# Twenty of the later modulation units moved from TensorE's stream to VectorE, in X's space

## The reference, cut to what matters

```
def adaln(cond, w, b):
    m = jax.nn.silu(cond) @ w + b            # w: (2048, 6 * 2048) per layer
    return six vectors of 2048: shift, scale, gate for the mixer and for the MLP
h  = modulate(x, g, shift, scale)            # rmsnorm(x, g) * (1 + scale) + shift
x  = x + gate * rmsnorm(mixer(h), g1)
m  = square(relu(modulate(x, ...) @ w1)) @ w2    # w1: 2048 x 8192, w2: 8192 x 2048
x  = x + gate * rmsnorm(m, g3)
```

## Time and profile before

| | |
|---|---|
| median of 3 runs | 2559.13 us (2557.03 to 2560.53) |
| profiled execution | 2560.89 us; its span 2559.1 us |
| TensorE busy (matmul) | 2497.7 us, 98% of the span |
| VectorE, ScalarE, GpSimd busy | 1364.3, 1050.2, 114.5 us |
| DMA moved | 634.51 MB, mean 248 GB/s |
| MLP0, MLP1 (first to last up-projection start and on) | about 560 to 1340 us, 1830 to 2559 us |

### The profile page before, as it was taken

The page is one execution under the profiler, slowest core; times in us unless marked ns, Lnnn a source line. Parts: engine busy times, 40 slices in busy tenths (PEclk is TensorE's granted clock), DMA queues, the critical chain, the costliest instruction groups (busy, mean ns, idle before and its releaser), DMA issues.

```text
span 2559.1 us, 37169 instructions
## 1 busy us (share of the span) xinstructions
PE 2497.7 (98%) x14658; PEld 2023.2 (79%) x14658; DVE 1364.3 (53%) x1492; ACT 1050.2 (41%) x1148; POOL 114.5 (4%) x164
## 2 busy tenths in 40 slices
PE   6899999989999999999999999999999999999998
PEld 3578888778778778778887777797787888888887
DVE  2244544475446545545565455565765465565565
ACT  3223334363333333333453365584633333343343
POOL 0020000000000000000000023200000000000000
PEclk8999999999999999999999999999999999999999
DMA  9989888958888887887867954457588555555554
GB/s 361 361 265 297 281 290 281 350 182 277 304 267 270 285 299 247 280 303 244 277 239 256 315 171 165 157 196 273 184 258 282 190 189 205 167 194 197 187 196 175
DMA packets 493365, 634.51 MB, mean 248 GB/s; under 512 B 12128, under 2 KB 370320, under 8 KB 491984
## 3 DMA queue, kind: packets, MB, share of 16 engines
q1 hardware_dynamic: 484576, 608.46, 71.3%
q0 software_dynamic: 6352, 23.31, 2.7%
q10 hardware_dynamic: 2336, 1.31, 0.2%
HBM read 623.90 MB, written 9.13 MB: 247 GB/s over the span
## 4 chain that ended last, share of the span: by engine, by line
PE 79%; DMA 10%; DVE 5%; ACT 4%; issue 2%; SPq 0%; ACTq 0%; DVEq 0%
PE PS L1301 23%; PE PS L1304 12%; PE PS L1371 11%; PE PS L1372 10%; PE PS L1373 10%; PE PS L1330 5%; DVE WLO L1864 3%; DMA RAW<-in_w_qkvg_gla 3%; ACT WHI L1608 2%; DMA RAW<-in_w_o_na 2%; DMA RAW<-in_w_o_gla 2%; DMA SCR<-in_w_ada 1%; DMA RAW<-in_w_qkv_na 1%; DMA RAW<-in_w_mlp 1%; PE PS L1484 1%
## 5 line engine op out<-in xcount | busy, mean ns | idle before, releaser
L1864 DVE TENSOR_TENSOR WLO<-RAW,WHI 128x2048 fp32r<-128x2048 f32 x384 | 879.1, 2300 | 776.1 <-ACT WHI L1608 767.4
L1608 ACT ACTIVATE WHI<-RAW 128x2048 fp32r<-128x2048 f32 x384 | 731.2, 1913 | 746.4 <-DMA RAW<-in_w_mlp 503.6
L1301 PE MATMUL PS<-HM,WHI 128*128 128x512 f32 x2560 | 650.8, 396 | 6.9 <-DVE SCR L2102 4.4
L1301 PEld LDWEIGHTS PS<-HM,WHI 128*128 128x128 f32 x2560 | 461.7, 189 | 105.8 <-issue 22.0
L1371 PE MATMUL PS<-WHI,HID 128*128 128x512 f32 x1152 | 454.0, 394 | 5.4 <-DVE WLO L1864 5.4
L1372 PE MATMUL PS<-WLO,HID 128*128 128x512 f32 x1152 | 449.7, 390 | 0.0
L1373 PE MATMUL PS<-WHI,HID 128*128 128x512 f32 x1152 | 449.1, 390 | 0.0
L1304 PEld LDWEIGHTS PS<-HM,WLO 128*128 128x128 f32 x2560 | 349.8, 191 | 25.8
L1304 PE MATMUL PS<-HM,WLO 128*128 128x256 f32 x2560 | 357.2, 283 | 0.0
L1371 PEld LDWEIGHTS PS<-WHI,HID 128*128 128x128 f32 x1152 | 216.6, 188 | 62.5 <-issue 17.9
L1373 PEld LDWEIGHTS PS<-WHI,HID 128*128 128x128 f32 x1152 | 216.8, 188 | 45.6
(11 more groups left out here) (239 smaller groups left out, 1691.5 us busy)
## 6 DMA issues: line engine op xcount, KB each, us to landing
RAW<-in_w_mlp SPq DMA_DIRECT2D x256, 1024.0 KB, 6.2
ADW<-in_w_ada SPq DMA_DIRECT2D x176, 1024.0 KB, 8.2
RAW<-in_w_qkv_na SPq DMA_DIRECT2D x48, 1024.0 KB, 7.1
RAW<-in_w_qkvg_gla SPq DMA_DIRECT2D x32, 1024.0 KB, 7.1
SCR<-in_w_ada SPq DMA_DIRECT2D x16, 1024.0 KB, 11.2
RAW<-in_w_o_na SPq DMA_DIRECT2D x16, 1024.0 KB, 7.2
RAW<-in_w_qkvg_gla SPq DMA_DIRECT2D x32, 512.0 KB, 4.7
RAW<-in_w_o_gla SPq DMA_DIRECT2D x16, 1024.0 KB, 6.5
```

What stands on the lines that cost most here:

```text
L1301: return mm(bank[:, 0:2 * T2], hi[:, k, P * b:P * b + P], act[:, kc, 0:2 * T2], start=first, stop=False)
L1608: actv(WHI[:, 2 * s + u, 0:n], RAW[:, u, 0:n], ACT.Copy).then_inc(hi_done, 1)
L1864: tt(WLO[:, 2 * s + u, 0:n], RAW[:, u, 0:n], WHI[:, 2 * s + u, 0:n].bitcast(f32), ALU.subtract).then_inc(lo_done, 1)
```

## The change

Units are still numbered 0 to 95, but 20 places among them are done in five "quads" of 4 units (1024 columns): after the out half's own units in groups 0, 1 and 2 of MLP0 and in groups 0 and 1 of MLP1. The last two quads overlap by one unit, so 19 different units leave TensorE's stream: 4 in the out half of each of groups 0 to 2 of MLP0, which keeps one unit in each of blocks 0 and 1, and all 7 of group 0 of MLP1. `ada` arguments become pairs (number in the stream, number of the unit), SKIP = 12 apart later on.

A quad q has 16 tiles of 128 rows by 1024 columns (512 KB). POOL loads each in two transfers of 256 KB into one of two slots, and VectorE multiplies it with the conditioning of its 128 rows, once for each vector, and adds it to two accumulators QACC (128 x 1024). Both the slots and the accumulators lie in X, which POOL parks in DRAM before and brings back after. TensorE sums QACC over the partitions with 8 matmuls, ACT copies and stores the rows.

```diff
+        PU = NB + 2
+        QU = 4
+        GU = PU + QU
+        QUADS0, QUADS1 = HID_GROUPS - 1, 2
-        PLAN_MLP = {GU: ((0, 1), (2, 3), (4,), (5,)), LU: ((0,), (1,), (2,), ())}
+        PLAN_MLP = ((0,), (1,), (), ())
+        QACC = [XF[:, QN * b:QN * b + QN] for b in range(2)]
+        QTILE = [XF[:, 2 * QN + QH * q:2 * QN + QH * q + QH] for q in range(2 * QN // QH)]
+        UP_TILES, OUT_TILES = 2 * NB, 2
+        QUAD_SLOT = [k % 2 for k in range(KC)]
...
         @block.tensor
...
+            def quad_rows(q):
+                pe.wait_ge(quad_step, q * KC + (KC + 1))
+                pe.wait_ge(quad_row, q + 1)
+                for b in range(2):
+                    for j in range(QU):
+                        end = mm(ROWS_TB[32 * j:32 * j + 32, 0:UC], PICK[b], QACC[b][:, UC * j:UC * j + UC],
+                                 start=(b == 0), stop=(b == 1))
+                end.then_inc(quad_summed, 1)
+                def between(n, x):
+                    planned_ada(None if a is None else g * PU + (a + NB), PLAN_MLP)(n, x)
+                    if quads is not None and n == YN - 1 and x == 2:
+                        quad_rows(g + quads)
...
         @block.scalar
...
+            def quad_store(q, unit):
+                act.wait_ge(quad_summed, q + 1)
+                act.wait_ge(quad_out, q * (16 * QU) + 16)
+                actv(QROW, ROWS_TB[:, 0:UC], ACT.Copy).then_inc(quad_row, 1)
+                act.wait_ge(quad_row, q + 2)
+                for j in range(QU):
+                    act.dma_start(mod_rows[ds(unit + j, 1)].rearrange("o h b j n -> (o b j) h n"),
+                                  QROW[32 * j:32 * j + 8, :].rearrange("p (h n) -> p h n", h=2)).then_inc(quad_out, 16)
...
         @block.vector
...
+            def quad_tile(q, k, slot, at):
+                dve.wait_ge(quad_zero, q * 2 + 2)
+                dve.wait_ge(quad_in[slot], q * (32 * PER_SLOT[slot]) + (at * 32 + 32))
+                dve.wait_ge(quad_step, q * KC + (k + 1))
+                for b in range(2):
+                    scale = CS[:, ds(k, 1), b:b + 1].rearrange("p o n -> p (o n)")
+                    end = nc.vector.scalar_tensor_tensor(QACC[b], QTILE[slot], scale, QACC[b], ALU.mult, ALU.add)
+                end.then_inc(quad_step, 1)
...
                 split_lo(m + 1, 1)
+                quad_out_tile(quad, n, 0)
...
                 split_lo(m + 2, 0)
+                for x in range(1, OUT_TILES):
+                    quad_out_tile(quad, n, x)
...
                     split_lo(slab + 1, 1 - s)
+                    if quad is not None:
+                        quad_tile(quad, i * 2 + s, s, i)
                     for b in range(2):
                         dve.wait_ge(hid_done, k + b + 1)
...
         @block.gpsimd
...
+            def quad(q):
+                if q:
+                    pool.wait_ge(quad_summed, q)
+                for b in range(2):
+                    nc.gpsimd.memset(QACC[b], 0.0).then_inc(quad_zero, 1)
+                for k in range(KC):
+                    slot, before = QUAD_SLOT[k], QUAD_BEFORE[k]
+                    if before is not None:
+                        pool.wait_ge(quad_step, KC * q + before + 2)
...
+                    for first, last in ((unit, middle), (middle, end)):
+                        at, col = (first - unit) * UC, first % edge * UC
+                        n = (last - first) * UC
+                        pool.dma_start(QTILE[slot][:, at:at + n],
+                                       w_ada[first // edge, P * k:P * k + P, col:col + n]).then_inc(quad_in[slot], 16)
+            def park_x(times):
+                pool.dma_start(x_park, XF).then_inc(x_parked, 16)
...
+                pool.wait_ge(x_parked, 16 * times)
+            def return_x(quads):
+                pool.wait_ge(quad_summed, quads)
+                pool.dma_start(XF, x_park).then_inc(x_back, 16)
                 nc.gpsimd.memset(SCR[:, 2 * S4:3 * S4], 0.0).then_inc(y_zero, 1)
+            park_x(1)
+            for q in range(QUADS0):
+                quad(q)
+            return_x(QUADS0)
```

More of the change, by code:

```diff
@@ L265, in build_program @@
         ROWSUM_T = CB[:, 1024:1024 + P]
+        QROW = CB[:, 1152:1152 + UC]
+        PICK = [CB[:, 1408 + 32 * b:1440 + 32 * b] for b in range(2)]
+        XF = X[:, :, :].rearrange("p b n -> p (b n)")
+        QN = QU * UC
+        QACC = [XF[:, QN * b:QN * b + QN] for b in range(2)]
+        QH = QN
+        QTILE = [XF[:, 2 * QN + QH * q:2 * QN + QH * q + QH] for q in range(2 * QN // QH)]
+        x_park = nc.dram_tensor("x_park", [P, 2 * D], f32, kind="Internal").ap()
+        quad_in = [sem(f"quad_in{q}") for q in range(2 * QN // QH)]
+        quad_step, quad_summed = sem("quad_step"), sem("quad_summed")
+        quad_row, quad_out = sem("quad_row"), sem("quad_out")
+        quad_zero = sem("quad_zero")
+        UP_TILES, OUT_TILES = 2 * NB, 2
+        QUAD_SLOT = [k % 2 for k in range(KC)]
+        QUAD_BEFORE = [max((p for p in range(k) if QUAD_SLOT[p] == QUAD_SLOT[k]), default=None) for k in range(KC)]
+        PER_SLOT = [QUAD_SLOT.count(s) for s in range(2)]
+        x_parked, x_back, pick_ready = sem("x_parked"), sem("x_back"), sem("pick_ready")
         NORM_OF = ((0, 0, 1, 2), (1, 0, 3, 5), (2, 1, 1, 2), (3, 1, 3, 5))
@@ L1644, in step @@
                 if ada is not None:
[L1645 to L1650, removed]
+                    store_row(*ada)
             def square(x, f, n, b):
@@ L1824, in mlp_group @@
                         slab = g * (4 * NB) + i * 2 + (m + s)
-                        ada = g * per + i + a if s == 0 and a is not None else None
+                        ada = (g * PU + i + a, g * GU + i + a) if s == 0 and a is not None else None
                         step(slab, s, ada, (g * KC + i * 4 + (layer * HID_GROUPS * KC + 2 * s), i, s))
@@ L1918, in cross, with quad_out_tile, out_slab @@
                                                ALU.mult, accum_out=ACC[:, XG, b, n:n + 1]).then_inc(crossed, 1)
-            def out_slab(m0, n, add, f=None, last=False, dst=Y, banks=YB):
+            def quad_tile(q, k, slot, at):
[6 more added lines that the diff above has]
+                end.then_inc(quad_step, 1)
+            def quad_out_tile(q, n, x):
+                if q is not None:
+                    k = UP_TILES + OUT_TILES * n + x
+                    quad_tile(q, k, QUAD_SLOT[k], QUAD_SLOT[:k].count(QUAD_SLOT[k]))
+            def out_slab(m0, n, add, f=None, last=False, dst=Y, banks=YB, quad=None):
                 m = m0 + 2 * n
                 split_lo(m + 1, 1)
+                quad_out_tile(quad, n, 0)
                 flush = FLUSH_AT.get((f, n))
@@ L2228, in _ @@
             nc.gpsimd.memset(SCR[:, 2 * S4:3 * S4], 0.0).then_inc(y_zero, 1)
+            park_x(2)
+            for q in range(QUADS0, QUADS0 + QUADS1):
+                quad(q)
+            return_x(QUADS0 + QUADS1)
             load_gain(3)
```

155 lines of the change are left out of this document (88 added, 67 removed).

## The result

The changed kernel takes **2588.97 us** (2587.61 to 2591.27, 4 runs) against 2558.98 us (4 runs) of the kernel before: ratio 1.0116 [1.0101, 1.0131], slower by 30 us. 2575 was forecast, and 2550 to 2595 as the range. The profiled execution took 2587.61 us, its span is 2585.8 us.

A forecast was written before the change was run, and what follows sets the result against it. TensorE, 98% busy, was taken as the bound. -39.3 + 5.2 + 13 + 12 + 3.4 + 22 = +16.3 us on the profiled 2560.89 us; against 2559.13 that gave 2575 us, range 2550 to 2595.

The forecast's parts named there:

- Rival 2: At two first tiles and five quad ends, loads less contended, waits summing to under 34 us: 2552 us; chance 0.22.
- Rival 4: Weight stream loses its lead; tiles delaying a split 1 us in every up slab add 40 us: about 2610 us; chance 0.08.
- Removed work: In TensorE's stream, 19 units' matmuls go at 2.07 us each: -39.3 us.
- `quad_rows`: +5.2: On TensorE, 8 matmuls of 256 columns per quad, 1.04 us with the entry, five times: +5.2 us.
- The tile: On VectorE, two merged operations per tile take about 2.5 us, bounds 2.4 and 3.0; 80 tiles, 200 us.
- First tiles: At each MLP's start, VectorE's first tile comes late and TensorE waits for `split_hi`: 13 us in MLP0, 12 in MLP1.
- Ends of quads: TensorE waits before `quad_rows` for tile 15: 5 us at three ends in MLP0, 3.5 at two in MLP1; 22 us.
- The clock: After each first-tile wait TensorE runs at 1.2 instead of 2.4 GHz, 1.7 us lost: +3.4 us, bounds 0 to 8.
- Up-half tiles: In up halves, tiles on VectorE are covered by its idle time, about 4 us per slab against 2.5: 0 us.

The follow-up runs named there:

- no_quads: The changed kernel with the quads left out and the 19 units' rows filled with other numbers: 2520.28 us.
- late_rows: The changed kernel with `quad_rows` after unit 3 of the last block instead of after unit 2: 2558.35 us.
- early_park: The changed kernel with X parked as soon as it is complete and a quad's first two tiles loaded ahead of the two memsets: 2571.07 us.
- tile_last: The changed kernel with the up half's tiles behind the split of the hidden values instead of between the weights' split and the halves: 2571.59 us.
- both: The changed kernel with late_rows and early_park together: 2545.77 us.
- both_tile_last: The kernel both, with the up half's tile moved behind the split of the hidden values: 2526.80 us.
- late_tile_last: The kernel late_rows, with the up half's tiles moved behind the split of the hidden values, park and memsets unchanged: 2543.77 us.

## Why the prediction was right, and where a term was off

**Direction and rival.** The forecast, that waits outweigh the matmuls, is what happened. Rival 2, loads less contended, falls: the waits at its seven places add up to 37.5 us, with the others to 42.6, against its limit of 34. It was close, though: 37.5 lies nearer to that limit than to the 47 forecast. Rival 4, a loss in every up slab, falls as it was put (the up halves of groups 1 and 2 cost nothing more in the kernel after), but its mechanism is real: see below.

**Removed work: -39.3.** Shown by no_quads, 39.5.

**`quad_rows`: +5.2.** 1.00 us from its start to the next matmul in three of the five, 1.87 and 1.86 in the two that fell into a stretch at the lower clock; in late_rows 1.00 all five times.

**The tile: 2.5 us.** 2.48 measured, within the bounds 2.4 to 3.0. (The "62.8, 42.3" read as shares of VectorE's time are microseconds: of 100.5 and 99.5 us they are 62.5 and 42.5%. And the up half's cover, 98 less 82.8, is 15 us, not 17. Neither moves the sum.)

**First tiles: +13 and +12.** 10.07 and 11.37 by the trace. Parking took 8.0 us from its issue (569.75 to 577.76) where 12 were reckoned, the first tile 7.8 from the first issue to VectorE's start (579.55 to 587.37) where 5.5 were: in all 2.7 us earlier than forecast. With early_park most of both goes.

**Ends of quads: +22.** 16.1, five waits of 3.0 to 3.6: the two at MLP1 were right (3.5), the three at MLP0 too high (5). early_park shows how loosely they hang: 5.7 and 6.1 there.

**The clock: +3.4. This is the term that was off most**, with its bounds "0 to 8, if the ends of quads bring it too". It was counted once per first tile, at 1.7. The table's last column has 14.6 us: 4.9 behind the two first tiles' waits, 8.0 behind four of the five ends, and 1.7 behind the wait of 3.49 us at the start of an out half, which the prediction did not have. With the 2.4 us that no window explains it is 17.0, short by 13.6. late_rows makes the case for the ends: 26.8 us for 16.1 us of waits. By the rule of the Trainium skill (TensorE: Matmul & The Clock Gate, Part 1) that speaks of idleness and half rate, the ends were put at 5 us more; the trace agrees with its sense at four of the five, and the price there was 8.0.

**Up-half tiles: 0, covered.** Half right, and only because larger waits stood beside them. Averages of VectorE's idle time (4 us per slab against 2.5) said there was room; the ring of dependencies has none. It showed in the kernel after as waits of 3.49 and 1.55 us at the starts of the out halves, 5.0 us that the prediction did not have; early_park left them, tile_last took them away. Once the other waits are gone the tile's place is worth 19 us (both against both_tile_last).

**Sum.** -39.3 + 5.2 + 21.4 (first tiles) + 16.1 (ends) + 5.0 (ring) + 17.0 (clock and the unexplained 2.4) + 1.2 elsewhere = +26.6, against +16.3 forecast. That the forecast came this near is in part luck: the seven waits were put 9.5 us too high (47 for 37.5), which hid part of what was missing, 13.6 of clock, 5.0 of the ring and 1.2 elsewhere. The other 3 us between 2575 and 2588.97 are the scatter of executions: the medians lie 30.0 apart, the profiled spans 26.7.

Taken away one after the other from 2588.97: place of `quad_rows` 30.6, place of the tiles 14.6, first tile 17.0 (late_rows, late_tile_last, both_tile_last), which leaves 2526.80. In another order the shares differ: the tile's place is worth 19 as the last step, the park 12.6 on late_rows.

**What would show it.** The 1952 matmuls, five waits before `quad_rows`, one at the third slab of each MLP, two of VectorE on POOL's DMA (24.6 us in all) and the pair of 2.5 us all came. "TensorE without gaps inside up halves" held except for the first tile's.

## What to carry to other kernels

Work moved to an engine with idle time is paid for by its place in that engine's queue: put it where the engine would wait for somebody else (here: for ACT's rounding and split), not between a result and the instruction that another engine waits for. When a wait on TensorE is priced, price the matmuls behind it at the lower clock too: here a pause of 3.0 to 3.6 us before `quad_rows` cost 4.7 to 6.7 where the clock fell. And when one wait is cured, look for it again downstream before counting the gain: of 35 us expected of early_park, 18 came.

## What the runs showed of the hardware that was not expected

**Short pauses of TensorE can bring the lower clock, and their length alone doesn't decide it.** After four of the five pauses of 3.0 to 3.6 us before `quad_rows` a window of 5 us showed a granted clock of 0.50 to 0.74, and the half cost 1.7 to 3.1 us beyond its pause. Pauses of 1.55 and 1.61 us (after, both) left it at 1.00; those of 1.88, 1.96 and 2.12 us had it in the windows behind them (0.83, 0.86, 0.80). One of 2.76 us (both, at 1847.58) and the one of 3.29 us at 766.25 (after) did not.

Two pairs show it best. At the start of MLP0's first out half a pause of 3.49 us (after, at 675.30) left a clock of 0.83 over the 10 us behind it, one of 3.52 us (early_park, at 663.87) left 1.00. And between the MLPs, where the kernels before and after have the same two pauses 6 us apart (1.67 and 1.46, 1.67 and 1.45 us), the 10 us behind them show 1.00 before (from 1356.92) and 0.83 after (from 1368.72). What else decides is open.
